# Loading the router's scores from the GpSimd queue in place of ScalarE's

## The reference

```python
q = (xb @ peer_wq).reshape(PEER_BLOCK, PEER_HEADS, 2, PEER_HALF)
s = jnp.einsum('thcd,hckd->thck', q, peer_sub_keys, preferred_element_type=jnp.float32)
s1, i1 = lax.top_k(s[:, :, 0], PEER_TOPK)
s2, i2 = lax.top_k(s[:, :, 1], PEER_TOPK)
...
top_s, top_pos = lax.top_k(cand_s, PEER_TOPK)
experts = jnp.take_along_axis(cand_i, top_pos, axis=-1)
g = jax.nn.softmax(top_s, axis=-1).astype(xb.dtype)
u = peer_u[experts]
act = jax.nn.gelu(jnp.einsum('thkd,td->thk', u, xb), approximate=False)
v = peer_v[experts]
return jnp.einsum('thk,thkd->td', g * act, v)
...
y = layer_norm(ALPHA * h + ff, ln2_g, ln2_b)
```

## Time and profile before

| | us |
|---|---|
| median of three executions | 3338.3 |
| the profiled execution, its own time | 3336.23 |
| its span | 3334.5 |
| PE busy | 2952.1 (89%) |
| DVE busy | 2391.4 (72%) |
| ACT busy | 1204.9 (36%) |
| POOL busy | 1502.0 (45%) |

### The profile page before, as it was taken

How to read it: one execution, slowest core, us unless ns; L and a number is a source line. 1 busy time by engine, 2 the same in 40 slices (tenths; PEclk the granted TensorE clock), 3 DMA queues, 4 the chain that set the end, 5 groups by cost and what they waited for, 6 DMA issues and landing times. The chain is left out here.

```text
span 3334.5 us, 35756 instructions
## 1 busy us (share of the span) xinstructions
PE 2952.1 (89%) x10191; PEld 1638.9 (49%) x10191; DVE 2391.4 (72%) x4846; ACT 1204.9 (36%) x3117; POOL 1502.0 (45%) x1114
## 2 busy tenths in 40 slices
PE   8988989776798898877688899999999999999993
PEld 5755655443445555444445555544444454544441
DVE  0021477797787867888767878778777788787787
ACT  0241233485733334775652422222222222222221
POOL 0000066665673667777888733333323333332330
PEclk9988999887798999888899899999999999999996
DMA  4576689878899999567699999999999999999995
GB/s 142 189 252 220 214 324 351 306 246 277 272 357 387 388 338 332 171 190 217 182 305 315 393 416 415 415 415 415 414 416 415 415 414 414 409 415 409 384 395 211
DMA packets 381189, 1096.91 MB, mean 329 GB/s; under 512 B 91616, under 2 KB 217792, under 8 KB 294848
## 3 DMA queue, kind: packets, MB, share of 16 engines
q0 software_dynamic: 161616, 741.61, 58.7%
q1 hardware_dynamic: 176800, 303.85, 25.6%
q10 hardware_dynamic: 42576, 49.17, 4.3%
HBM read 1031.18 MB, written 62.23 MB: 328 GB/s over the span
## 5 line engine op out<-in xcount | busy, mean ns | idle before, releaser
L467 POOL DMA_INDIRECT expert_rows<-in_experts,picked_index x525 | 613.1, 1168 | 873.0 <-DVE ff_sum L621 749.6
L490 POOL DMA_INDIRECT gates_by_expert<-dense_gate,gate_address x384 | 687.5, 1790 | 213.2 <-issue 114.8
L609 DVE SCALAR_TENSOR_TENSOR expert_rows<-expert_rows,h_tile 128x1024 f32<-128x1024 f32 x557 | 678.3, 1218 | 135.4 <-DMA expert_rows<-in_experts,picked_index 115.8
L621 DVE SCALAR_TENSOR_TENSOR ff_sum<-expert_rows,coefficients,ff_sum 128x1024 f32<-128x1024 f32 x557 | 713.1, 1280 | 31.2 <-ACT coefficients L572 30.4
L1849 PE MATMUL dense_out_ps<-dense_value_rows,dense_weights 128*128 128x512 f32 x1536 | 688.5, 598 | 39.0 <-DVE dense_weights L1927 39.0
L1860 PE MATMUL dense_act_ps<-dense_hT,key_columns 128*128 128x384 f32 x2048 | 691.3, 491 | 19.2 <-DMA key_columns<-in_key_columns 13.2
L1860 PEld LDWEIGHTS dense_act_ps<-dense_hT,key_columns 128*128 128x128 f32 x2048 | 386.5, 191 | 337.4 <-DMA key_columns<-in_key_columns 60.1
L1849 PEld LDWEIGHTS dense_out_ps<-dense_value_rows,dense_weights 128*128 128x128 f32 x1536 | 293.7, 192 | 388.4 <-issue 311.1
L878 PE MATMUL proj_ps<-xT,w_in_block 128*128 128x384 f32 (+1 forms) x1392 | 422.3, 466 | 26.9 <-DMA xT<-in_xT 11.8
L566 ACT ACTIVATE activated<-dots 128x1 f32<-128x1 f32 (+1 forms) x629 | 125.8, 200 | 671.4 <-DVE expert_rows L609 496.5
L878 PEld LDWEIGHTS proj_ps<-xT,w_in_block 128*128 128x128 f32 x1392 | 268.0, 193 | 180.6 <-issue 32.8
(11 more groups left out here) (198 smaller groups left out, 3069.8 us busy)
## 6 DMA issues: line engine op xcount, KB each, us to landing
key_columns<-in_key_columns SPq DMA_DIRECT2D x128, 512.0 KB
dense_value_rows<-in_experts SPq DMA_DIRECT2D x128, 512.0 KB
gates_by_expert<-zeros POOLq DMA_DIRECT2D x12, 2048.0 KB, 21.9
wq_half<-in_peer_wq SPq DMA_DIRECT2D x48, 512.0 KB, 11.4
dense_gates<-gates_by_expert SPq DMA_DIRECT2D x128, 192.0 KB
w_in_block<-in_w_in ACTq DMA_DIRECT2D x18, 1024.0 KB
w_in_block<-in_w_in SPq DMA_DIRECT2D x18, 1024.0 KB
w_out<-in_w_out SPq DMA_DIRECT2D x24, 512.0 KB, 7.4
```

What stands on the lines that cost most here:

```text
L467: pool.indirect_dma_start(to, None, self.a["experts"], bass.IndirectOffsetOnAxis(ap=index[:, k:k + 1], axis=0)).then_inc(got, 16)
L490: pool.indirect_dma_start(self.a["gates_by_expert"], bass.IndirectOffsetOnAxis(ap=self.flat[i][:, k:k + 1], axis=0), self.dgate[i][:, k:k ...
L609: dve.scalar_tensor_tensor(place, place, 1.0, self.h[n % 2][:], ALU.mult, ALU.mult, accum_out=self.dots[:, s % TOPK:s % TOPK + 1]).then_in ...
L621: dve.scalar_tensor_tensor(total, self.slots[self.slot_of[p]][:, D:2 * D], self.coef[:, y % TOPK:y % TOPK + 1], total, ALU.mult, ALU.add). ...
```

## The change

The 66 loads of scores leave ScalarE's queue. `lay_out_loads` gives each a place in GpSimd's list: route r is loaded at the event where route r - 1 begins, but not before the stage scores of the route's own group (of a later group: its first route event there). `pool` issues it there, ahead of what that event has for GpSimd. The two waits and the DMA itself stay as they are, on the new engine. ScalarE's bookkeeping (`stored`, `loaded`, `softmaxed`) goes.

```diff
         key = lambda k: (points[k][0], points[k][1])
-        self.h_at, self.scatter_at = {}, {}
+        self.scores_at, self.h_at, self.scatter_at = {}, {}, {}
+        for r, (t, h) in enumerate(self.routes):
+            k = max(k_of["route", r - 1, 0] if r >= 2 else 0, opened[home[t]])
+            assert k <= k_of["route", r, 0], (r, t, h)
+            self.scores_at.setdefault(key(k), []).append(r)
...
             elif e[2] == self.SOFTMAX_AFTER:
                 self.act_softmax(self.nc.scalar, e[1])
-                self.softmaxed = e[1]
-                self.load_scores(self.nc.scalar)
...
         for i, e in enumerate(self.events):
+            for r in self.scores_at.get((self.block, i), []):
+                self.load_scores(pool, r)
             for n in self.h_at.get((self.block, i), []):
                 self.load_h(pool, n)
...
-    def load_scores(self, act):
-
-        while self.loaded < min(self.softmaxed + 3, len(self.routes)):
-            t, h = self.routes[self.loaded]
-            if (t, h if t != SAMPLE else h + 3) not in self.stored:
-                return
-            self.load_score(act, self.loaded)
-            self.loaded += 1
-
-    def load_score(self, act, r):
+    def load_scores(self, pool, r):
         t, h = self.routes[r]
         if r >= 2:
-            act.wait_ge(self.fine, self.count[r - 2, 1])
+            pool.wait_ge(self.fine, self.count[r - 2, 1])
...
-            act.wait_ge(self.m["scores_stored"][n % SCORE_STAGES], 16 * (n // SCORE_STAGES + 1))
-        act.dma_start(self.sc[r % 2][:].rearrange("p c n -> p (c n)"), self.a["peer_scores"][t * HEADS + h]).then_inc(self.sc_in[r % 2], 16)
+            pool.wait_ge(self.m["scores_stored"][n % SCORE_STAGES], 16 * (n // SCORE_STAGES + 1))
+        pool.dma_start(self.sc[r % 2][:].rearrange("p c n -> p (c n)"), self.a["peer_scores"][t * HEADS + h]).then_inc(self.sc_in[r % 2], 16)
...
                         nc.scalar.copy(qT[h % 2][:, c, :], qp[2 * (h % 2) + c][:, 0:W]).then_inc(q_copied, 1)
-                        if c == 0:
-                            bg.stored |= {(t, h - 2) for t in g.tiles}
-                            bg.load_scores(act)
                         bg.act(part(h + 0.45 * (c + 1)))
```

More of the change, by code:

```diff
@@ L239, in __init__ @@
         self.table = None
-        self.stored, self.loaded, self.softmaxed = set(), 0, -1
     def lay_out(self):
@@ L387, in act @@
                 self.act_rows(self.nc.scalar, range(e[1], e[1] + e[2]))
-            elif e[2] == 0:
-                assert self.loaded > e[1], (self.block, e, self.loaded)
             elif e[2] == self.SOFTMAX_AFTER:
                 self.act_softmax(self.nc.scalar, e[1])
-                self.softmaxed = e[1]
-                self.load_scores(self.nc.scalar)
             elif e[2] == self.INDEX_AFTER:
@@ L1740, in _ @@
                         nc.scalar.copy(qT[h % 2][:, c, :], qp[2 * (h % 2) + c][:, 0:W]).then_inc(q_copied, 1)
-                        if c == 0:
-                            bg.stored |= {(t, h - 2) for t in g.tiles}
-                            bg.load_scores(act)
                         bg.act(part(h + 0.45 * (c + 1)))
-                else:
-                    bg.stored |= {(t, h - 2) for t in g.tiles}
                 if h >= 1:
@@ L1756, in _ @@
                         bg.act(part(h + 0.92 + 0.03 * x))
-            bg.stored |= {(t, HEADS - 1) for t in g.tiles}
             bg.act(1.0)
```

## The result

| | before | after |
|---|---|---|
| median of six runs, us | 3338.45 (3336.23 to 3345.68) | 3362.57 (3360.93 to 3365.89) |
| profiled execution, us (span) | 3336.23 (3334.5) | 3362.38 (3360.6) |

The ratio is 1.0066, 95% interval 1.0056 to 1.0077: the change makes the kernel slower, by 24.1 us between the medians and by 22 (19 to 26) by the ratio. The forecast was 3351 with a range of 3336 to 3368. The sign and the range held. The size was some 12 us short by the medians, 9 by the ratio.

The account below looks back on a forecast made before the run. GpSimd was taken to bound mla 3 and transfers the stage dense; 1.7 + 3 + 5 + 6 + 0 - 2 = +13.7 us on 3336.2 gave 3349.9, as a median 3352.0. It said 3351, range 3336 to 3368.

Parts of the forecast that it names:

- all ahead of mla_project 3 (scores 1, group 2, ...): Before mla_project 3: loads not hidden by GpSimd's waits cost +1.7 us in scores 1 and +3 in group 2's stages.
- mla_project 3, mla 3, merge 3: Seven loads where GpSimd is behind: five in mla 3 cost 4.3 us, two at the edges 0.7; term +5.
- scores 3: Route 42's load is issued late, VectorE starts 9.8 us later, some four are taken back: +6 us.
- dense: Last stage: its 20 loads fit where GpSimd waits for VectorE, and its bytes don't change: term 0.
- ScalarE's side: Over the kernel: ScalarE is relieved of 22 us of issue and its waits for stores, taken as -2 us.
- Price of a load: On GpSimd's list: one load costs 0.86 us, median 0.56 plus 0.30 between instructions; bounds 0.80 and 1.53.
- The port lock: On GpSimd: VectorE's hold on shared ports makes descriptors wait, 1.53 us a load, 3359 in all; chance 0.05.
- VectorE's later starts: In mla 3: late loads make VectorE stand 3 us, but it then waits less for rows; nothing added.
- if the stage dense moves: Sign against the forecast: dense leaving 1421.7 us by over 2 would mean loads touch a bound put at nothing.
- It all hides: Rival, whole kernel: waits shrink to absorb the loads, leaving +2 us, 3340; chance 0.25.
- The loads queue up: Rival: full stages land loads after 15 us or more, half the middle stages' 24 us shows: +33, 3371; chance 0.15.

Follow-up runs that it names:

- e1: The changed kernel with the loads of routes 42 and 43 back on ScalarE, the other 64 on GpSimd: 3349.87 us, ratio 1.0032.
- e4: The kernel before, score loads still on ScalarE, plus 66 unused loads of 128 8-byte rows on GpSimd at the changed kernel's places: 3348.42 us, ratio 1.0022.
- e5: The changed kernel with each load nearly a route earlier in GpSimd's list, except routes 42 and 43: 3376.71 us, ratio 1.011.
- e7: The changed kernel with route 42's load alone three events further up GpSimd's list: 3353.47 us, ratio 1.0046.
- e2: The kernel before with only the 20 loads of the stage dense moved to GpSimd: 3340.49 us, ratio 0.9996.
- e6: The kernel before with only the loads of routes 42 and 43 moved to GpSimd: 3354.61 us, ratio 1.0049.
- e11: The kernel before with 19 DRAM copies of 512 KB added in dense on ScalarE's queue, 10 MB in all: 3366.24 us, ratio 1.0073.
- e3: The kernel before with only the five loads issued in mla 3 (routes 37 to 41) moved to GpSimd: 3345.7 us, ratio 1.0017.
- e9: The kernel before with 16 scatters moved out of mla 3, eight to project 3 and eight to stick 3: 3325.3 us, ratio 0.9957.
- e10: The kernel before with eight scatters moved out of mla 3 to project 3: 3328.91 us, ratio 0.9971.

## Why the prediction was right, and where its size was wrong

| step | forecast | between the two traces |
|---|---|---|
| all ahead of mla_project 3 (scores 1, group 2, ...) | +4.7 | +3.1 at the start of mla_project 3 (1493.2, 1496.3) |
| mla_project 3, mla 3, merge 3 | +5 | +9.1 |
| scores 3 | +6 | +7.5 |
| dense | 0 | +6.5 |
| ScalarE's side | -2 | not to be seen |
| sum | +13.7 | +26.2 |

**Price of a load: near, and too high.** The row of L432 says 940 ns and 1.2 us in most of the records, not the 0.56 that I said the profile would show. The timeline tells why that isn't its cost:

```profile
1632.77 2.60 POOL L482 DMA_INDIRECT gates_by_expert<-dense_gate,gate_address  x1 [0.30 <-issue]
1634.80 1.22 POOL L432 DMA_DIRECT2D expert_scores<-peer_scores  x1
1636.31 1.59 POOL L482 DMA_INDIRECT gates_by_expert<-dense_gate,gate_address  x1 [0.30 <-issue]
```

The load's record begins at 1634.80, while the scatter ahead ends at 1635.37. Between that end and the next start lie 1636.31 - 1635.37 = 0.94 us. Of these, 0.30 stand between two of POOL's instructions without a load too, so the load adds 0.64 us; the other four loads of the stage add 0.65 or 0.66. I had 0.86, because I counted that gap to the load. The port lock, the rival with a chance of 0.05 at 1.53 us a load, is not borne out: the long records are overlap. The Trainium skill (Perfetto Trace Analysis, DMA Instruction — SWDGE (GPSIMD)) says that such a record has no start of its own and ends when the last descriptor is written; the overlapping row fits that.

**Scores 1 and the middle: within the noise.** 2.7 us in scores 1, and 3.1 up to mla_project 3, where the start of mla 3 alone spreads over 6.6 us with the loads unmoved.

**Mla 3: right mechanism, half of the size open.** GpSimd again waits for nobody there. 8.4 us for my 4.3: seen over all traces, mla 3 + merge 3 is 269.8 to 273.1 with all of GpSimd's loads up to there (after, e1, e4, e5, e7; mean 271.3) and 261.4 to 267.6 without them in the same table of scatters (before, e2, e6, e11; mean 263.9). That is +7.4, and not the 8.8 of the first two traces; e3, with the stage's own loads alone, has 268.0. GpSimd's list in mla 3, before (L490, L467) and after (count, then busy us and mean ns):

```profile
L490 POOL DMA_INDIRECT gates_by_expert<-dense_gate,gate_address x60 | 103.6, 1727 | 18.3 <-issue 18.0 <-POOLq L1108 0.3
L467 POOL DMA_INDIRECT expert_rows<-in_experts,picked_index x27 | 29.8, 1104 | 8.2 <-issue 8.2
...
L482 POOL DMA_INDIRECT gates_by_expert<-dense_gate,gate_address x62 | 106.6, 1720 | 18.9 <-issue 18.6 <-POOLq L1100 0.3
L459 POOL DMA_INDIRECT expert_rows<-in_experts,picked_index x27 | 31.0, 1146 | 8.2 <-issue 8.2
```

The five loads add 3.2 us of the 8.4. Two more scatters start in the stage, 3.6 us with their gaps, and the same 27 gathers take 1.2 longer. The two scatters are not carried in: when mla 3 starts, GpSimd has issued 259 scatters and 226 gathers in both traces. So the stage ended a little further on in GpSimd's list than before, and its list is not all that sets the end. What the rest is, no run takes apart. VectorE's later starts, which I had at nothing, can't be all of it, since e4 has none and grows as much.

**Scores 3: the step that failed.** "DVE starts 9.8 us later than before ... 9.8 less some four". The first half was too small. It waited 14.1 us longer (19.21 for 5.08), because 12 us and not 6.7 went by from the issue to the start. Four of it were to be taken back by later waits; between these two traces nothing was. The stage shows only 7.5 of the 14 us, which looks like a saving; against e1, e2 and e3 (110.0 to 111.0) it shows 11.

**Dense: the other half of the same step.** "The stage dense is bound by transfers ... and these bytes don't change." The first clause is right (e11), the second is wrong. The total of the kernel doesn't change, but where it is moved does. Bytes that scores 3 did not move while VectorE and GpSimd stood, 2.76 MB of them, were moved in dense, and dense paid 6.6 us. 7.5 + 6.5 = 14.0 us against 14.1 us of VectorE's added wait: one for one in this pair of traces. In e6's trace 9.9 us stand against 14.4, while its ratio says 16, so "one for one" is known to some 4 us. I had named this myself as what would prove me wrong, "if the stage dense moves". In the traces e1 takes the 14 away with two loads, e7 most of them with one load's place (scores 3 + dense 1537.0); by the ratios it is 11 and 7.

**ScalarE's -2.** No run shows a gain: e1, which has nearly all of ScalarE's relief, is above e4, which has none (10.7 and 7.3, intervals overlapping).

**The rivals.** "It all hides" failed on mla 3 and on scores 3. "The loads queue up" (3371) was nearer than I gave it credit for: its late landing is what happened, at one route; but its 12 us for the middle stages did not come, since all ahead of mla_project 3 was 3.1. By the rule that I cited from the Trainium skill (DMA: Bandwidth & Descriptors, SWDGE vs HWDGE vs iDMA) the landing on GpSimd's queue would be later than 6.7 us in the full stages. In three traces it was (after, e5, e6: 11.9 to 12.1 us from the start of the record, 11.3 to 11.5 from the end of the scatter ahead), in e7, on the same queue and with DMA just as full, it was 7.3, and on ScalarE's 7.3 as well (1830.14 to 1837.42). So the queue alone is not the cause.

**Still open:** what makes those 12 us out of 7.3. In the three slow cases GpSimd issued nothing, or only further loads, behind the load; in e7 a gather followed at once. No run takes that apart.

## What to carry to other kernels

An engine's added work has the price of the stage it stands in: nothing where the engine waits for a free buffer (16 scatters, 20 loads), and over half of its time where it waits for nobody (16 scatters: 19 of 32 us). If the last stage is bound by bytes, a stall ahead of it is not forgiven: read the bytes moved in each stage, not the total, and add what is put off. And when work moves to an in-order queue, look at the first item of a batch, whose data has just been made: late by 14 us it cost some 14 us (7 to 16 over the runs that move it), and put too early in the same queue it cost as much again.

## What the runs showed of the hardware

- A plain load of 128 rows of 1 KB adds 0.65 us to GpSimd's list where it runs back to back, and so does one of 8-byte rows (e4: its record ends 0.65 us behind the scatter ahead). With 8-byte rows mla 3 + merge 3 was 273.1, no less than with 1 KB rows (269.8 to 271.5).
- DRAM-to-DRAM copies of 10 MB, spread over dense, cost 24 us, and the stage's mean rate stayed at 399 GB/s beside 400: they cost what the same bytes cost as loads into SBUF.
- The long stall has a small second price. PE's granted clock in the changed kernel from 1852 on: full (1.00, the 2.4 GHz level) while it worked, 0.50 (1.2 GHz) after it had run dry, still 0.50 when it worked again, and full in the window from 1880. Over the stage PE's busy time for the same 352 matmuls was 100.33 us for 99.97.

```profile
1852.00:1858.00 6.00, 6.00 (x22) 3.63 (x21) 0.00 (x0) 0.00 (x0) 2.44 (x4) 1.00 1.08 419
1858.00:1864.00 6.00, 0.65 (x6) 0.46 (x5) 0.00 (x0) 0.00 (x0) 0.00 (x0) 0.99 1.06 387
1864.00:1870.00 6.00, 0.00 (x0) 0.00 (x0) 5.77 (x22) 0.50 (x2) 1.01 (x1) 0.50 1.08 363
...
1872.00:1876.00 4.00, 4.00 (x10) 2.48 (x10) 3.79 (x13) 2.20 (x6) 2.78 (x4) 0.50 1.07 405
...
1880.00:1884.00 4.00, 4.00 (x14) 2.37 (x13) 4.00 (x5) 2.01 (x6) 3.10 (x3) 1.00 0.98 251
```

In mla 3 the granted clock rose as the stage got shorter: 0.81, and 0.90 in e9, where PE was busy 97.01 us for the same 600 matmuls instead of 106.76. Whether that is a part of the 19 us of e9 is not shown: e10 won 11 us at 0.82, and in e11 PE was busy 110.68 us at 0.79 while the stage took 158.3, no longer than before.
